# Another beginning, and another order of work around three attentions, in a two-block kernel on one core

## The reference

```
for layer in 0, 1:                                   # f0, f1
    h = rms_norm(x, norm_w[layer]); proj = h @ w_in[layer]      # 1024 x 5376
    a = sliding_window_attention(rope(q), rope(k), v, sinks) * silu(z)   # 8 heads of 64
    b = rms(hgrn2_recurrence(silu(qh), kin, i, logf)) * silu(g)          # chunks of 64
    x = x + (sigmoid(ga) * (a @ w_up_attn) + sigmoid(gh) * (b @ w_up_hgrn)) @ w_out
x = rms_norm(x, final_norm_w)
mod = silu(c) @ ada_w + ada_b                        # 2 x 6 x 1024
s0: y = dsa_mixer(h): q, ckv, iq, ik, iw = h @ w_in; 16 heads; keys = ckv @ w_uk, values = ckv @ w_uv,
        softmax over the 64 keys that iq, ik, iw choose; @ w_o
s1: y = squared-relu MLP, 1024 -> 4096 -> 1024
s2: y = differential attention, 8 heads of 2 x 64, @ w_o
s3: y = MLP;   after each: x = layer_norm(alpha x + (1 + gate) y)
```

## Time and profile before

| | us |
|---|---|
| median of 3 runs | 1145.67 |
| lowest and highest of them | 1145.09, 1146.24 |
| profiled execution, its own time | 1146.26 |
| span of that execution | 1144.5 |

### The profile page before, as it was taken

One profiled execution on the slowest core, in us unless ns is written; L12 is line 12 of the kernel. 1 busy time (PEld: TensorE's weight loads), 2 busy tenths in 40 slices (PEclk: granted clock), 3 DMA queues, 4 the chain that ended last, 5 costly groups with the idle time before them and its releaser, 6 DMA issues.

```text
span 1144.5 us, 16781 instructions
## 1 busy us (share of the span) xinstructions
PE 1070.6 (94%) x6634; PEld 900.7 (79%) x6634; DVE 485.5 (42%) x747; ACT 549.8 (48%) x771; POOL 832.7 (73%) x685
## 2 busy tenths in 40 slices
PE   5899999999799999998899999999999699999996
PEld 5778878787588787796678888996887379989994
DVE  5646444246654443474745222006524645230015
ACT  4643557456335574544634443443445335444442
POOL 5997766879776668671057998887786157999995
PEclk9999999999899999999999999999999899999999
DMA  7647633555377336854765767964666824565750
GB/s 249 201 137 288 228 122 116 181 182 166 105 263 233 117 120 165 308 161 138 294 215 172 237 220 276 338 193 147 206 227 229 312 84 134 176 195 184 225 161 38
DMA packets 112804, 221.65 MB, mean 194 GB/s; under 512 B 14944, under 2 KB 21462, under 8 KB 112726
## 3 DMA queue, kind: packets, MB, share of 16 engines
q1 hardware_dynamic: 107552, 210.30, 55.5%
q10 hardware_dynamic: 5174, 10.28, 2.5%
HBM read 219.48 MB, written 1.07 MB: 193 GB/s over the span
## 4 chain that ended last, share of the span: by engine, by line
PE 71%; POOL 9%; DVE 9%; ACT 4%; issue 3%; DMA 2%; ACTq 0%; DVEq 0%; SPq 0%; POOLq 0%
PE lin_ps L358 12%; PE lin_ps L360 11%; PE lin_ps L359 11%; POOL wlo L1024 9%; PE tmp_ps L365 5%; PE tmp_ps L367 5%; PE tmp_ps L366 5%; PE tmp_ps L552 3%; PE tmp_ps L653 3%; PE lin_ps L365 3%; PE lin_ps L367 3%; PE lin_ps L366 3%; ACT whi L1142 2%; PE tmp_ps L422 2%; PE lin_ps L589 1%
## 5 line engine op out<-in xcount | busy, mean ns | idle before, releaser
L1024 POOL TENSOR_TENSOR wlo<-ring,whi 128x512 fp32r<-128x512 f32 (+2 forms) x608 | 795.0, 1338 | 256.6 <-ACT whi L1142 246.8
L1142 ACT CAST whi<-ring 128x1024 fp32r<-128x1024 f32 (+2 forms) x304 | 312.6, 1034 | 412.0 <-PE lin_ps L360 224.8
L358 PE MATMUL lin_ps<-whi,hThi 128*128 128x512 f32 (+2 forms) x528 | 208.5, 395 | 13.7 <-POOL wlo L1024 8.3
L359 PE MATMUL lin_ps<-wlo,hThi 128*128 128x512 f32 (+2 forms) x528 | 201.9, 382 | 0.0
L360 PE MATMUL lin_ps<-whi,hTlo 128*128 128x512 f32 (+2 forms) x528 | 201.6, 382 | 0.0
L365 PE MATMUL tmp_ps<-hThi,whi 128*128 128x256 f32 x520 | 147.5, 284 | 0.1
L367 PE MATMUL tmp_ps<-hThi,wlo 128*128 128x256 f32 x520 | 147.1, 283 | 0.0
L366 PE MATMUL tmp_ps<-hTlo,whi 128*128 128x256 f32 x520 | 147.1, 283 | 0.0
L358 PEld LDWEIGHTS lin_ps<-whi,hThi 128*128 128x128 f32 x528 | 99.9, 189 | 48.4 <-POOL wlo L1024 15.0
L360 PEld LDWEIGHTS lin_ps<-whi,hTlo 128*128 128x128 f32 x528 | 100.0, 189 | 19.7
L1938 DVE TENSOR_TENSOR arena<-tmp_ps,arena 128x1024 f32<-128x1024 f32 x16 | 19.6, 1224 | 222.4 <-ACT arena L1369 222.4
(11 more groups left out here) (288 smaller groups left out, 1471.4 us busy)
## 6 DMA issues: line engine op xcount, KB each, us to landing
ring<-in_mlp_w SPq DMA_DIRECT2D x128, 512.0 KB, 4.4
ring<-in_ada_w SPq DMA_DIRECT2D x82, 512.0 KB, 4.8
ring<-in_w_in SPq DMA_DIRECT2D x80, 512.0 KB, 4.8
ring<-in_b_w_in SPq DMA_DIRECT2D x24, 512.0 KB, 4.5
ring<-in_w_out SPq DMA_DIRECT2D x16, 512.0 KB, 3.4
arena<-in_ada_w SPq DMA_DIRECT2D x27, 256.0 KB, 5.4
ring<-in_a_w_in SPq DMA_DIRECT2D x12, 512.0 KB, 7.4
ring<-in_w_up_hgrn SPq DMA_DIRECT2D x8, 512.0 KB, 3.5
```

What stands on the lines that cost most here:

```text
L358: pe.matmul(ps, xh, hi, start=first, stop=False, skip_group_check=True)
L359: pe.matmul(ps, xh, lo, start=False, stop=False, skip_group_check=True)
L1024: pool.tensor_tensor(wlo[:, n % PARTS, cut, 0:width], source[:, cut, :], whi[:, n % PARTS, cut, 0:width].bitcast(F32), ALU.subtract).then_ ...
L1142: act.copy(whi[:, n % PARTS, :, 0:width], ring[:, u % RING, 2 * h:2 * h + 2, 0:width]).then_inc(S("high_formed"), 1)
```

## The change

Start: SP issues the nine small loads and waits for x before any ring unit, so that x is loaded alone; positions, sinks and lambda are issued by SP between units 1 and 2; relT, the one-hot table and final_norm_w by ACT after the first operand. `warm` is copied from `ones`. The norm goes tile by tile through ACT, DVE and POOL; two halves are cast ahead of the operand, not three; 6 constant products in place of 14. The level masks are formed by DVE after `hTlo` and by POOL after the lows of four halves. f0 and f1: gh0 goes to the other half of `lin_ps`. s0: the transposes of w_uk stand between q0 and q1; only K's first half is computed ahead of the attention, V and K's second half within its first two quads; w_uk's slot is given back at K's sixth of eight pairs; slab 26 waits for V's second tile. s2: k1 goes to the other half; the sums are closed at n = 2 and there are no slabs at 4, 5, 6 but two at 7 and two at 8; output_turned(0) comes after n = 9; w_o's first part is followed by four slabs, the closing and output_turned(1).

```diff
...
+BUSY = {"f0": 6, "f1": 4, "s0": 4, "s1": 0, "s2": 0, "s3": 12}
...
-FIRST_STAGED = {1: (26, 3, "s0k1"), 5: (27, 0, "s0s3"), 7: (28, 1, "s0s7")}
+FIRST_STAGED = {1: (26, 3, "s0v1"), 5: (27, 0, "s0s3"), 7: (28, 1, "s0s7")}
...
-                    feature_major("f0hT", hs, ready=(S("f_scaled"), 1), busy=BUSY["f0"])
+                    turned_by_tiles("f0", hs, S("f_scaled"), 0, None, range(4))
...
+                def gates(name, first, k0, other=False):
...
+                          {0: [gates("ga1", GA0 + HALF, 4)], 1: [gates("gh0", GH0, 0, True), gates("gh0", GH0, 4)],
...
+                if behind is None:
+                    ada_close()
...
+                            mid=None if behind else (lambda: output_turned(name, 1)))
+                if behind:
+                    behind()
+                    output_turned(name, 1)
...
-            for n in range(2):
-                linear_feat(f"s0q{n}", w, n * HALF, hT)
-
+            linear_feat("s0q0", w, 0, hT)
             slot = take((slice(0, HALF), I["a_w_uk_2"][0].rearrange("h d r -> (h d) r").rearrange(
...
-            wait_read("s0ckvT")
-            slot = take((0, "wuv"), (1, "wuv"))
...
-                if i == 0:
...
-                else:
-                    finished("s0v1", used(mm))
-            wait_read("s0wuk0", "s0wuk1")
-            for h in range(2):
+            linear_feat("s0q1", w, HALF, hT)
...
                 ps = open_tmp(f"s0k{h}")
...
+                    if h == 0 and c == 2:
+                        used(mm)
                 close_tmp(mm, f"s0k{h}")
-            wait_read("s0q0", "s0q1", "s0k0", "s0k1", "s0v0", "s0v1")
+
+            wait_read("s0ckvT", "s0wuk0", "s0wuk1")
+            keys_of(0)
...
+                def part(half):
+                    if i == 0:
+                        slot = take((0, "wuv"), (1, "wuv"))
+                        uv.append(slot.rearrange("p a b -> p (a b)").rearrange("p (r n) -> p r n", r=2))
+                    ps = open_lin(f"s0v{i}", 1 - half if i else half)
...
+                            mm = pe.matmul(ps[:, c, :], ckvT[:, r, i * P:(i + 1) * P], uv[0][:, r, c * HALF:(c + 1) * HALF],
...
+                        finished("s0v0", (S("s0v0_full"), 1))
...
+            wait_read("s0q0", "s0q1", "s0k0")
...
-            reserve(HALF, (slice(0, HALF), win(I["a_w_o_2"][0], 0, HALF, 0)))
...
                       lambda b, head: vv[:, b, head * HD:(head + 1) * HD], HD, QUAD, (Pq_second, pT_second),
-                      {10: [lambda half: output_turned("s0", 0)]}, lag=2,
-                      after={n: (lambda n=n: (ada(2), stage_first(n))) for n in ADA_QUADS})
+                      {0: [values_of(0)], 1: [values_of(1)],
+                       3: [lambda half: wait_read("s0v0", "s0v1", "s0k1")], 10: [lambda half: output_turned("s0", 0)]},
+                      lag=2, after={0: lambda: keys_of(1),
+                                    **{n: (lambda n=n: (ada(2), stage_first(n))) for n in ADA_QUADS}})
...
-                feat_units("s2k1", open_lin("s2k1", half), w, D + HALF, hT)
+                feat_units("s2k1", open_lin("s2k1", 1 - half), w, D + HALF, hT)
...
                       {0: [queries], 1: [slabs_between(2), keys], 2: [values(0), landed("s2v0")],
                        3: [values(4), landed("s2q1", "s2k1")],
-                       6: [landed("s2v1")], 10: [lambda half: output_turned("s2", 0)]}, lag=2,
-                      after={4: lambda: (reserve(HALF, (slice(0, HALF), win(I["b_w_o_2"][0], 0, HALF, 0))), ada(4)),
-                             5: lambda: ada(2), 6: lambda: ada(2)})
-            project("s2", I["b_w_o_2"][0])
+                       6: [landed("s2v1")]}, lag=2,
+                      after={2: ada_close, 7: lambda: (reserve(HALF, (slice(0, HALF), win(I["b_w_o_2"][0], 0, HALF, 0))), ada(2)),
+                             8: lambda: ada(2), 9: lambda: output_turned("s2", 0)})
+            project("s2", I["b_w_o_2"][0], lambda: (ada(2), ada(2), ada_close()))
...
+            rows = 0
...
+                      I["c_2"].rearrange("b (k p) -> (b k) p", p=P)):
+                sp.dma_start(stackA[rows:rows + v.shape[0], :], v).then_inc(S("small_landed"), 16)
...
+            sp.wait_ge(S("x_landed"), 16)
             for n, unit in enumerate(units):
-                if n == 1:
-
-                    sp.wait_ge(S("x_landed"), 16)
+                if n == 2:
+                    sp.dma_start(posi[:], I["positions"].rearrange("b (i p) -> p (b i)", p=P),
...
+                                  I["b_lambda_2"].rearrange("l a d -> (l a d)").partition_broadcast(P)
+                                  ).then_inc(S("lamb_landed"), 16)
...
-            pool.affine_select(out=levelmask[:, 1:, :], in_=levelmask[:, 1:, :], compare_op=ALU.is_gt, fill=0.0,
-                               base=0, pattern=[[0, LEVELS - 1], [1, P]], channel_multiplier=-1
-                               ).then_inc(S("levels"), 1)
...
             row, one = st[:, 1, :, 0], st[:, 2, :, 0]
-            rstd("f0", row, one)
-            pool.wait_ge(S("f_scaled"), 1)
+            for i in range(NT):
+                pool.wait_ge(S("f0var"), i + 1)
+                pool.tensor_tensor(one[:, i:i + 1], row[:, i:i + 1], half[:, i, 0:1], ALU.pow).then_inc(S("f0rstd"), 1)
+            pool.wait_ge(S("f_scaled"), NT)
+            lows(LEVELMASK_BEHIND, 0)
+            pool.wait_ge(S("levels_both"), 1)
+            pool.affine_select(out=levelmask[:, 1:, :], in_=levelmask[:, 1:, :], compare_op=ALU.is_gt, fill=0.0,
+                               base=0, pattern=[[0, LEVELS - 1], [1, P]], channel_multiplier=-1
+                               ).then_inc(S("levels"), 1)
             rotate(0)
             rstd("f0h", st[:, 1], st[:, 2], "f0ho")
-            tile_rstd("f0", (S("f_scaled"), 1 + NT), row)
...
             act.dma_start(x[:], I["x"].rearrange("b (i p) d -> p (b i) d", p=P)).then_inc(S("x_landed"), 16)
-            rows = 0
-            for v in (I["norm_w"].rearrange("l (k p) -> (l k) p", p=P),
...
-            act.dma_start(posi[:], I["positions"].rearrange("b (i p) -> p (b i)", p=P),
-                          allow_slow_non_contiguous=True).then_inc(S("posi_landed"), 16)
...
-            def high_of(name, k0, cols=None):
-
-                ps = flat(full_tmp(name))
+            def high_of(name, k0, cols=None, lead=True):
+
+                if lead:
+                    ahead(name)
+                ps = flat(full_tmp_of(act, name))
...
-            act.wait_ge(S("relT_ones"), 1)
-            act.dma_start(relT[0:NBUCKET, :], I["rel_bias_2"]).then_inc(S("rel_landed"), 16)
...
-            act.wait_ge(S("chunkmask"), 1)
-            act.copy(warm[:], chunkmask[:, 0:HALF]).then_inc(S("warm"), 1)
+            act.wait_ge(S("ones"), 1)
+            act.copy(warm[:].rearrange("p (a b) -> p a b", a=4), ones[:].unsqueeze(1).broadcast_to([P, 4, P])
...
-                        ins = act.activation(hs[:, i, :], x[:, i, :], ACT.Square, accum_out=st[:, 0, i, 0:1])
-                    ins.then_inc(S("f0ss"), 1)
-                    high_parts(PARTS, 0)
+                        act.activation(hs[:, i, :], x[:, i, :], ACT.Square, accum_out=st[:, 0, i, 0:1]
+                                       ).then_inc(S("f0ss"), 1)
+                    high_parts(2, 0)
...
                 if L == 0:
+                    ahead("f0hT1")
+                    act.wait_ge(S("relT_ones"), 1)
+                    act.dma_start(relT[0:NBUCKET, :], I["rel_bias_2"]).then_inc(S("rel_landed"), 16)
+                    act.dma_start(onehot, I["onehot"]).then_inc(S("rel_landed"), 16)
+                    act.dma_start(lnp[:, 0, :], I["final_norm_w"].partition_broadcast(P)).then_inc(S("lnp_landed"), 32)
                     ahead("f0hT1", 1)
                     act.wait_ge(S("lb_max"), 1)
...
+            queries_read(0)
             for r in range(2):
                 ps = full_tmp(f"s0wuk{r}")
                 read(act.copy(wukT[:, r, :], flat(ps)), f"s0wuk{r}")
...
-                ps = full_tmp(f"s0k{h}")
-                read(act.copy(flat(kT[:, 4 * h:4 * h + 4, :]), flat(ps)), f"s0k{h}")
+            queries_read(1)
+            keys_read(0)
...
-            attention("s0", quads, QUAD, (Pq_second, pT_second), lag=2, no_lead=tuple(range(10)))
+            attention("s0", quads, QUAD, (Pq_second, pT_second),
+                      evacuate={0: lambda: values_read(0), 1: lambda: keys_read(1), 2: lambda: values_read(1)},
+                      lag=2, no_lead=tuple(range(10)))
...
-            dve.wait_ge(S("pairs"), 1)
-            step(dve.tensor_tensor(pairx[:, 0, :], pairx[:, 0, :], pairx[:, 1, :], ALU.bitwise_xor))
...
-            dve.tensor_tensor(levelmask[:, 1:, :], levelge[:, 1:LEVELS, :], levelge[:, 2:, :], ALU.subtract
-                              ).then_inc(S("levels_both"), 1)
...
-                    variance("f0", st[:, 0, :, 0], st[:, 1, :, 0], D, EPS)
-                    dve.wait_ge(S("f0rstd"), 1)
```

(36 more changed lines are left out.)

80 lines of the change are left out of this document (37 added, 43 removed).

## The result

The changed kernel took 1153.09 us in the median of four runs (1151.28 to 1154.36), the kernel before on the same chip 1145.95: a ratio of 1.0059, 95% interval 1.0045 to 1.0073, so 5 to 8 us slower. The forecast, 1147.3 and no change to speak of, was wrong, and 1153.09 lies above its range.

The account below looks back on a forecast made before the run. The prediction took TensorE, busy 1070.6 of 1144.5 us, as the bound. Start +1.4, attention of both first blocks -1.7, s0 +4.6 and s2 -2.7 summed to +1.6 on the median 1145.67: 1147.3 us, range 1140.8 to 1151.4.

Parts of the forecast that it names:

- s0: Stage with reordered K and V: late w_uv, late slab and slow clock cost +4.6 us (ends -1.8 and +6).
- s2: Stage with moved slabs: DVE paces the quads, y0's second part starts earlier, -2.7 us (ends -6 and +1).
- The halves: Attention of f0 and f1: gh0 in the other lin_ps half shortens waits, 0.84 twice, -1.7 us (ends -2.1 and 0).
- The beginning: Kernel start: earlier high parts, but level masks in DVE's chain delay the last cast, +1.4 us (ends -2.5 and +3.4).
- the level operations: DVE's level masks at the start: 3.5 us alone plus three holds of 1.3 behind POOL's lows, 7.4 us.
- some 1.5 us to come and go: Start: allowance added to 3.6 us of transfer for x loaded alone, giving about 5.8 us in all.
- the 1.05 of k1: In s2: the wait of 1.05 us at 869.23 goes when k1 takes the other half.
- a hole before V: In s0: w_uv's load waits for w_uk's slot and lands at 530.0, so PE stands 3.2 us.
- the term of the late slab: In s0: staged slab waits for V1, ring slabs move 5.8 us, second slab ends at 553.9, worth +1.8 us.
- The 1.4 for V's clock: In s0: half of the 2.8 us that a lower granted clock behind the hole would cost, +1.4 us.
- 4.4 less 1.7: In s2: y0's second part 4.4 us earlier at full clock, 1.7 given back for a slower clock between quads.
- Rival C: PE's clock falls in s0's hole and between s2's quads: s0 +6.0, s2 +0, 1151.4 us; chance 0.33 with its halves.

Follow-up runs that it names:

- e5: Kernel before with the new beginning alone: 1145.47 us, ratio 0.9995 to the kernel before.
- e2: Changed kernel with DVE's twelve level operations back ahead of the norm: 1152.97 us, ratio 1.0052 to the kernel before.
- e9: Changed kernel with s0 in its old order, DVE's masks first and s2's second half turned ahead of the slabs: 1140.69 us, ratio 0.9953 to the kernel before.
- e14: Kernel before with the new beginning (DVE's masks first) and the swaps of halves, s0 and s2 as before: 1140.58 us, ratio 0.9941.
- e15: The same file as e9, measured a second time: 1140.94 us, ratio 0.9951 to the kernel before.
- e10: Kernel before with the swaps of lin_ps halves alone (gh0 in f0 and f1, k1 in s2): 1142.94 us, ratio 0.9973.
- e3: Changed kernel with s2's second half turned ahead of the four slabs: 1151.90 us, ratio 1.0048 to the kernel before.
- e8: Changed kernel with slab 26 not staged but coming through the ring: 1164.94 us, ratio 1.0174 to the kernel before.
- e11: Kernel before with the new s0 alone: 1156.18 us, ratio 1.0089 to the kernel before.
- e13: The changed kernel, unaltered, measured again: 1157.50 us, ratio 1.0103 to the kernel before.
- e4: Changed kernel with w_uv ahead of w_o in the ring: 1152.28 us, ratio 1.0049 to the kernel before.

## Why the prediction was wrong

The forecast was +1.6 us and the profile gives +7.6. Three places make the miss: s0, mis-sized by 2.8; s2, wrong in sign, 3.5 off; and the index products, 1.45, for which there was no term. The halves add 1.4 to it. The beginning (0.8), k1 (1.1) and the stretch at 313 us (1.2) take some of it back.

**The beginning (+1.4): right in its mechanism.** The cast came at 32.01 (forecast 32.9), the level operations took 7.1 us in the chain (7.4), the high parts started at 12.31 (12.6), the first product at 14.28 (14.6). The "some 1.5 us to come and go" in x's load no run shows by itself; x landed 5.33 us after its issue, at 6.13 (5.8). The term was +0.56 in the profile and -0.6 by e5's time (-1.8 to +0.7): no loss and no gain. Putting the masks first (e2, e9, e14, e15) moved the cast by 2.7 us, not by the whole 7.1. The Trainium skill's rule on the shared port pair ("SBUF — State Buffer", "Who interferes with whom") in its strict reading would have let the one-input operations pass. The seven comparisons and the cast to f32, with one input each, took 3.1 and 0.6 us longer beside POOL's lows than alone. The Trainium skill also says there that such operations can enter a two-port mode and then contend. That part the trace bears out.

**The halves (-1.7 and the 1.05 of k1): the waits right, the worth in the two layers too large.** gh0's wait fell from 1.46 to 1.19 and gh1's went. Timeline of PE in f0 (answers to the earlier trace rows):

```profile
149.96 0.50 PE L359 MATMUL lin_ps<-whi,hThi 128*128 128x512 f32 x1 [1.19 <-DVE hs L1768]
```

But of the 0.84 for each layer 0.17 went to a new wait for POOL's lows, and 0.5 came back where later transposes wait 1.44 for ACT's copy of the last probabilities and waited 0.95 before. Each layer gained 0.17 by matched products, 0.3 us together where the forecast had 1.7. k1's 1.1 stayed whole. Alone, the three swaps measured 3.1 us of gain (1.8 to 4.4), more than these 1.4; where the rest is, the one trace of e10 does not tell.

**s0 (+4.6, measured 7.4): the first step that failed, by its size.** Its order of events was right: w_uv issued at the sixth pair (524.67, forecast 524.6 with the shift of 0.56), a hole before V (3.8 us, forecast 3.2), a slab late in quad 3. The 2.8 us too little lie in the term of the late slab, "the second waits to 552.9 and ends at 553.9". With the shift of 0.56 and the 1.4 for the clock that is 555.9; it ended at 558.64.
- Its second half was issued at 547.58, 1.3 us later than those numbers give: w_uv's second half landed at 531.25 (forecast 530.6), and V's tiles take 3.7 and not 3.5. SP waits for V's second tile before the staged slab, so all of it comes on top.
- From issue to landing it took 9.43 us, where I took 8.62, the time of the same half before. The whole burst grew likewise, from a median of 8.8 to 9.8.
- Its products took 1.49 us and not 0.96, since the wait for the DMA itself brought the clock down (0.70 over them). I had charged the hole before V with a slow clock and no other one.

The 1.4 for V's clock, "I take half of it", fits this execution (5.07 - 3.70 = 1.4), and that was luck. Six traces have the hole before V; in the five others (e2, e3, e8, e11, e13) the tile took 6.31 to 6.69 us at a granted clock of 0.55 to 0.58, a loss of 2.6 to 3.0, the whole of the 2.8 worked out from the earlier trace rows. The Trainium skill's rule in "TensorE: Matmul & The Clock Gate", Part 1, that the slow clock is the resting state, weighed against the half that I took. The traces bear it out: behind the hole V's tile ran at 0.55 to 0.71, and the products behind the waits for the slabs' DMA at 0.50 to 0.70. So s0 cost 9.2 in e2 and e11, 8.5 in e3 and 10.5 in e13.

**The index products (no term, +1.45).** They stand ahead of s0's q0 and are not in the 7.4. They took 3.46 us before and 4.91 here, at a clock of 0.66, with no edit near them. In all seventeen traces of this case the same wait of 0.83 us stands before them; they took 3.46 us in nine and 4.7 to 5.0 in eight, and the moment at which PE gets there does not sort them (492.70 us was fast, 492.72 slow). I had put no term on work that is only shifted.

**s2 (-2.7, measured +0.8 without k1): the second step that failed, in sign.** The term is 4.4 less 1.7; the 1.05 of k1, named in front of it, is in neither, and with it the same numbers give -3.75 and a forecast of 1146.2. The times below are those of the trace less the 6.8 us by which PE comes later to this stage.
- "transposes 923.4; y0's second part starts at about 925.5" left out what stands between: the transposes themselves at the lower clock (1.93 us), ACT's high and DVE's low parts of that half, and 2.74 us of waiting. Before, this was hidden in the middle of y0's first part. y0's second part started at 927.9, 2.0 us earlier than before and not 4.4.
- Behind that wait the first products of y0's second part ran at a clock of 0.50, and 2.8 us went there. I had given 1.7 back for the clock between the quads, and nothing at this place. The two together turn -4.4 into +0.8; the four traces with the turning first take most of it back.
- The base: in the stage the profiled execution of before was a slow one. The same four slabs took 5.34 us in it and 3.64 in e5, e10, e11 and e14, whose s2 has the old order, and the stage was 1.5 to 3.0 us shorter in these. Timeline of PE in e5:

```profile
887.88 3.64 PE L553 MATMUL tmp_ps<-ring,csil 128*32 128x512 f32 x32
...
909.73 1.12 PE L423 MATMUL tmp_ps<-ident,arena 128*128 128x128 f32 x4 [4.75 <-DVE arena L2062]
```

The wait for DVE is there too, 4.75 us, and the stage is short all the same. Against such traces even the mended order gained nothing (-2.2 against -2.0).

The last combination came at 906.6 (913.4 in the trace) and the forecast had 905.5. But the 912.04 that it was set against is the combination of the quad before; the last one ended at 915.28 in the kernel before.

The sum by the parts, from the times: -0.6 -3.1 +10.2 +2.4, where the forecast had +1.4, -1.7, +4.6 and -2.7. Rival C (1151.4) named the clock as the cause in s0 and in s2 and is nearest. Its s0 has the size of V's loss but not that of the slab. In s2 the clock did fall between the quads (the two slabs of quad 7 took 3.61 us at 0.53 and not 1.92), but most of the loss stands behind the turning.

What remains open: why V's tile runs at 0.71 in one execution and at 0.55 to 0.58 in five, and what decides about the index products. The gains of e9 and e14 (5.4 and 6.8 us by their ratios) are larger than e5's and e10's together (3.7) by 2 to 3 us. The masks first fit that size, with products 2.1 to 2.4 us ahead behind f1's attention, but they were not run with the beginning alone. Nor was the new s0 run with w_uv early and both slabs of quad 3 in time, so that whether its order is worth anything by itself is not shown; e4's 0.5 us up to scores(2) is all that the traces have.

## What to carry to other kernels

A transfer that waits for a slot of the ring gets its start from the product that frees the slot: when work is reordered, count ring positions for every load. w_uv here needed to be one place earlier, and moving it there made a slab behind it late in its turn. What was turned, split or copied in the shadow of products must keep a shadow when it moves. A term taken from one execution in a stage with a clock below 1 should be checked against a second trace of the same code. And every new hole, a wait for a DMA or for DVE as much as an empty queue, should be asked for the slow products behind it: here they cost 0.5 to 3.0 us for each. A cost taken as half of its bound may fit one execution and miss the next five.

## What was not expected of the hardware

The granted clock falls in places that the edit does not touch. The same 32 index products behind the same wait of 0.83 us took 3.46 us at 1.00 or 4.7 to 5.0 (4.91 at 0.66). Such falls can make gains of 1 to 2 us in this kernel appear and vanish. Two measurements of the changed file differ by 4.4 us in their medians, while those of the kernel before stay within 0.4. In the two profiled executions, 3.4 us apart, the clock at V's tile and behind the slabs is the difference in s0 (10.5 against 7.4).
